# Transposing by VectorE blocks and GpSimd transfers in place of TensorE, halves-first FFN chunks, and keys and queries with the weights stationary, in a two-layer decoder trunk

## The reference

```
x = x + 0.5 * swiglu_ffn(rmsnorm(x, norm_ffn1[l]), ffn1_w_in[l], ffn1_w_out[l])      # 1024 -> 2 x 2816 -> 1024
z = rmsnorm(x, norm_mix[l]) @ mix_w_in[l]         # 2048 columns, split among four mixers A, B, C, D
x = x + concat(y_a, y_b, y_c, y_d) @ mix_w_out[l]
# cross attention, 4 heads of 256, 256 memory rows:
q = (rmsnorm(x, norm_xattn[l]) @ wq);  k, v = split(rmsnorm(mem, norm_mem[l]) @ wkv)
p = softmax(q k^T / sqrt(256));  x = x + (p v) @ wo
x = x + 0.5 * swiglu_ffn(rmsnorm(x, norm_ffn2[l]), ffn2_w_in[l], ffn2_w_out[l])
```

## Time and profile before

| | |
|---|---|
| median of 3 runs | 1118.09 us (1118.0 to 1118.31) |
| the profiled execution | 1116.31 us |
| its span | 1114.6 us |
| PE busy | 1101.6 us, 99% |
| DVE busy | 705.2 us, 63% |
| ACT busy | 541.7 us, 49% |
| POOL busy | 371.5 us, 33% |
| clock granted to TensorE | 1.0 but in the first and the last slice of 40 |

### The profile page before, as it was taken

One profiled execution on the slowest core, in us unless ns is written; L12 is line 12 of the kernel. 1 busy time (PEld: TensorE's weight loads), 2 busy tenths in 40 slices (PEclk: granted clock), 3 DMA queues, 4 the chain that ended last, 5 costly groups with the idle time before them and its releaser, 6 DMA issues.

```text
span 1114.6 us, 13351 instructions
## 1 busy us (share of the span) xinstructions
PE 1101.6 (99%) x4998; PEld 911.9 (82%) x4998; DVE 705.2 (63%) x811; ACT 541.7 (49%) x599; POOL 371.5 (33%) x727
## 2 busy tenths in 40 slices
PE   8999999999999999999999999999999999999996
PEld 7888888888888888888888888888888888888885
DVE  6666655799655655654565656468986557666552
ACT  6454534845554544443454535357464545444431
POOL 0686820000000056773017767000000002676610
PEclk9999999999999999999999999999999999999998
DMA  8977565644553477766567676556454436766561
GB/s 261 298 231 210 188 218 175 216 158 135 206 189 98 131 230 223 216 214 198 187 201 220 212 227 197 187 189 205 144 184 168 165 116 193 214 213 217 190 206 62
DMA packets 181792, 214.29 MB, mean 192 GB/s; under 512 B 18186, under 2 KB 137558, under 8 KB 181728
## 3 DMA queue, kind: packets, MB, share of 16 engines
q1 hardware_dynamic: 158112, 200.82, 55.8%
q0 software_dynamic: 22528, 11.58, 3.9%
q10 hardware_dynamic: 1088, 1.05, 0.3%
HBM read 200.79 MB, written 1.05 MB: 181 GB/s over the span
## 4 chain that ended last, share of the span: by engine, by line
PE 88%; issue 5%; ACT 2%; DVE 2%; DMA 1%; POOL 1%; DVEq 0%; SPq 0%; POOLq 0%; ACTq 0%
PE acc L1291 27%; PE acc L1293 27%; PE acc L1292 27%; PE turn L1189 3%; PE acc L1484 1%; PE acc L1459 1%; DMA w_raw<-in_ffn_w_in 1%; ACT w_hi L423 1%; DVE w_lo L751 1%; POOL kT L388 1%; DVE arena L955 1%; PE acc L1262 0%; PE acc L1386 0%; PE acc L1263 0%; PE acc L1273 0%
## 5 line engine op out<-in xcount | busy, mean ns | idle before, releaser
L751 DVE TENSOR_TENSOR w_lo<-w_raw,w_hi 128x2048 fp32r<-128x2048 f32 x191 | 428.0, 2246 | 231.4 <-ACT w_hi L423 231.2
L423 ACT CAST w_hi<-w_raw 128x2048 fp32r<-128x2048 f32 x191 | 357.2, 1871 | 128.7 <-PE acc L1293 114.8
L388 POOL DMA_DIRECT2D kT<-kT x704 | 344.2, 497 | 161.0 <-DVE kT L862 117.9
L1291 PE MATMUL acc<-w_hi,xT_hi 128*128 128x512 f32 x872 | 342.3, 393 | 0.0
L1293 PE MATMUL acc<-w_hi,xT_lo 128*128 128x512 f32 x872 | 339.7, 390 | 0.0
L1292 PE MATMUL acc<-w_lo,xT_hi 128*128 128x512 f32 x872 | 339.3, 389 | 0.0
L1291 PE MATMUL acc<-w_hi,hT_hi 128*128 128x512 f32 x608 | 240.7, 396 | 0.8 <-DVE hT_lo L940 0.8
L1293 PE MATMUL acc<-w_hi,hT_lo 128*128 128x512 f32 x608 | 237.1, 390 | 0.0
L1292 PE MATMUL acc<-w_lo,hT_hi 128*128 128x512 f32 x608 | 236.6, 389 | 0.0
L379 POOL TENSOR_TENSOR rstd<-var,mhalf 128x2 f32<-128x2 f32 x14 | 24.2, 1730 | 575.5 <-DVE var L788 428.1
L1293 PEld LDWEIGHTS acc<-w_hi,xT_lo 128*128 128x128 f32 x872 | 163.7, 188 | 34.6
(11 more groups left out here) (111 smaller groups left out, 500.8 us busy)
## 6 DMA issues: line engine op xcount, KB each, us to landing
w_raw<-in_ffn_w_in SPq DMA_DIRECT2D x174, 512.0 KB, 5.0
...
```

Of the source, the lines that this page charges most:

```text
L388: pool.dma_start(hfeat[B * q:B * q + B, g % 2, a * RUN:(a + 1) * RUN], hblk[B * a:B * a + B, g % 2, q * RUN:(q + 1) * RUN]).then_inc(hfeat ...
L423: act.copy(w_hi[:, u % SLOTS, 0:n], w_raw[:, u % SLOTS, 0:n]).then_inc(w_split_hi, 1)
L751: dve.tensor_tensor(w_lo[:, u % SLOTS, 0:n], w_raw[:, u % SLOTS, 0:n], w_hi[:, u % SLOTS, 0:n].bitcast(F32), ALU.subtract).then_inc(w_spli ...
L1291: pe.matmul(o, hi, wh, start=(first and j == 0), stop=False)
```

## The change

It has four parts.

1. **Twelve turns of the residual go** (`mi00`, `mi01`, `f2in10`, `f2in11` in both layers, `next00`, `next01`, and layer 1's `start10`, `start11`). In their place VectorE transposes `xs` in blocks (`x_blocks`), GpSimd issues 16 transfers of 32 rows of 1024 bytes (`x_shuffle`) for the half, and VectorE multiplies what landed by the gain (`gained_blocks`). `xblk` and `xfeat` are the memory that `hblk` and `hfeat` use, and waits keep them apart. The other boundary turns stay.
2. **Chunks 0 to 2 of an FFN go by halves**, but for the very first FFN: TensorE does half 0 of chunks 0, 1, 2 and then half 1 of each (`in_order`, `unit_of`; the loads follow). Each chunk's split of hidden features (`hidden_hi`, `hidden_lo`) comes one chunk later in the lists.
3. **Keys and queries are computed with the weights stationary** (`unit_t`): 48 matmuls of 256 columns instead of 24 of 512; the result has features on partitions, so the 16 turns of keys and queries and ScalarE's copies of them go. The second token tile of a half is needed with the first.
4. Since a row's scale can't be applied there any more, **the memory is scaled once at the start** (two VectorE operations in chunk 5 of the first FFN; the turns of `sgu_w` now stand ahead of the memory's), and the queries' scale goes into the softmax's scale (`qscale`) and its maximum.

```diff
+    def staged(l, f):
+        return (l, f) != (0, 0)
+
+    def unit_of(base, l, f, c, j):
+        if staged(l, f) and c < 3:
+            return base + 3 * j + c
+        return base + 2 * c + j
+
+    def in_order(l, f):
+        if staged(l, f):
+            return [(c, j) for j in range(2) for c in range(3)] + [(c, j) for c in range(3, FC) for j in range(2)]
+        return [(c, j) for c in range(FC) for j in range(2)]
...
     def layer_turns(l):
-        return ([f"start1{t}" for t in range(T)] + chunk_turns(l, 0) + [f"mi{n}{t}" for n, t in part]
-                + ["glu", "am", "b", "w", "u", "k00", "k01", "k10", "k11", "conv", "norm"]
-                + [f"q_in{n}{t}" for n, t in part] + ["q00", "q01", "q10", "q11"]
+        return (([] if l else [f"start1{t}" for t in range(T)]) + chunk_turns(l, 0) + [f"mi1{t}" for t in range(T)]
+                + ["glu", "am", "b", "w", "u", "conv", "norm"]
+                + [f"q_in{n}{t}" for n, t in part]
                 + ["p0", "p1", "p2", "p3"]
-                + [f"f2in{n}{t}" for n, t in part] + chunk_turns(l, 1)
-                + ([f"next0{t}" for t in range(T)] if l < L - 1 else []))
+                + [f"f2in0{t}" for t in range(T)] + chunk_turns(l, 1))
...
-        xT_hi = sb("xT_hi", [P, KT, S], F32R)
-        xT_lo = sb("xT_lo", [P, KT, S], F32R)
-        hT_hi = sb("hT_hi", [P, FT, S], F32R)
-        hT_lo = sb("hT_lo", [P, FT, S], F32R)
+        xT = sb("xT", [P, KT, 2, S], F32R)
+        hT = sb("hT", [P, FT, 2, S], F32R)
+        xT_hi, xT_lo = xT[:, :, 0, :], xT[:, :, 1, :]
+        hT_hi, hT_lo = hT[:, :, 0, :], hT[:, :, 1, :]
...
+        xblk, xfeat = kT[:, 0:4, :].rearrange("p k s -> p (k s)"), kT[:, 4:8, :].rearrange("p k s -> p (k s)")
...
+            def x_shuffle(h):
+
+                pool.wait_ge(xblk_ready, T * (h + 1))
+                pool.wait_ge(hT_ready, 1 + chunks_past(h))
+                if h:
+                    pool.wait_ge(xg_ready, xg_count(h - 1))
+                for a in range(NBLK):
+                    for q in range(NBLK):
+                        pool.dma_start(xfeat[B * q:B * q + B, a * XRUN:(a + 1) * XRUN],
+                                       xblk[B * a:B * a + B, q * XRUN:(q + 1) * XRUN]).then_inc(xfeat_landed, 16)
...
+                x_shuffle(x_half(l, 1, 0))
+                for k, i in enumerate((V_MIX, V_SGU, V_CLN, V_Q)):
                     inv_sqrt(at.at(6, 3 + k), i)
+                x_shuffle(x_half(l, 3, 1))
+                inv_sqrt(at.at(6, 7), V_F2)
                 for c in range(FC):
...
-                                       scale=rstd[:, V_MEM, t:t + 1]).then_inc(k_ready, 1)
-
-                def key_turn(n):
-                    for t in range(T):
-                        act.wait_ge(turned, turn_no(at.l, f"k{n}{t}"))
-                        act.copy(kT[:, 4 * n:4 * n + 4, t * P:(t + 1) * P],
-                                 tb[TB[f"k{n}{t}"]][:, :].rearrange("p (k s) -> p k s", k=4)).then_inc(kT_ready, 1)
+                    for c in range(2):
+                        evac(U_K + 2 * n + 1, c)
+                        act.copy(kT[:, 4 * n + 2 * c:4 * n + 2 * c + 2, :],
+                                 acc[KPAIR][c][:, :].rearrange("p (k s) -> p k s", k=2)).then_inc(kT_ready, 1)
...
-                    if (l, f) == (0, 0) and 3 <= c < 7:
+                    weights_to(base + (6 + c if staged(l, f) and c < 2 else 2 * c + 4), at)
...
+            def x_blocks(l, b, n, t):
+
+                h = x_half(l, b, n)
+                dve.wait_ge(x_updated, 16 * l + (T + 4 * (b - 1) + 2 * n + t + 1 if b else 2 * n + t + 1 - 2))
+                if h:
+                    dve.wait_ge(xfeat_landed, 16 * NBLK * NBLK * h)
+                for g in range(max(0, chunks_past(h) - 2), chunks_past(h)):
+                    dve.wait_ge(hfeat_landed[g % 2], hfeat_count(g))
+                dve.transpose(xblk.rearrange("p (q k t s) -> p t k q s", q=NBLK, k=4, t=T)[:, t, :, :, :],
+                              xs[:, t, n * GN:(n + 1) * GN].rearrange("p (k q s) -> p k q s", k=4, q=NBLK)).then_inc(xblk_ready, 1)
+
+            def gained_blocks(l, b, n, g):
+
+                h = x_half(l, b, n)
+                dve.wait_ge(xfeat_landed, 16 * NBLK * NBLK * (h + 1))
+                gain = par_all[:, l, g * KT + 4 * n:g * KT + 4 * n + 4].unsqueeze(2).unsqueeze(3).to_broadcast([P, 4, NBLK, B])
+                for t in range(T):
+                    dve.tensor_tensor(xg[:, t, :].rearrange("p (k a s) -> p k a s", k=4, a=NBLK),
+                                      xfeat.rearrange("p (a k t s) -> p t k a s", a=NBLK, k=4, t=T)[:, t, :, :, :],
+                                      gain, ALU.mult).then_inc(xg_ready, 1)

...
-                    split_lo(base + 2 * c + 5, at)
-                    if (l, f) == (0, 0) and c == 7:
+                    if c >= 2:
+                        hidden_lo(c - 2)
...
+                    if (l, f) == (0, 0) and c == 5:
+                        dve.wait_ge(rstd_ready, 2)
+                        for t in range(T):
+                            dve.tensor_scalar(mem_sb[:, t, :], mem_sb[:, t, :], rstd[:, V_MEM, t:t + 1], None, ALU.mult).then_inc(mem_scaled, 1)
...
+                    if b == 2:
+                        weights_to(u_end + 4, at)
+                        for t in range(T):
+                            update(b, 1, t, u_end + 2, pairs[1], factor, at)
+                            x_blocks(l, 3, 1, t)
+                        dve.wait_ge(x_squared, at.at(16, 8 + 4 * (b + 1)))
+                        variance(i_var, steps)
+                        weights_to(u_end + 6, at)
+                        gained_blocks(l, 3, 1, g)
+                        for t in range(T):
+                            xT_lo_part(b + 1, 1, t, at)
+                        return
...
-                    dve.tensor_scalar(nmax[:, h, :], smax[:, h, :], -SCALE, None, ALU.mult).then_inc(nmax_ready, 1)
+                    dve.scalar_tensor_tensor(out=nmax[:, h, :], in0=smax[:, h, :], scalar=-SCALE, in1=rstd[:, V_Q, :],
+                                             op0=ALU.mult, op1=ALU.mult).then_inc(nmax_ready, 1)
...
+            def unit_t(u, at, pair, s, k0, first, last, between=None):
+
+                pe.wait_ge(w_split, at.at(UNITS, SLOTS + u + 1))
+                slot = u % SLOTS
+                for c in range(GN // P):
+                    o = acc[pair][c // 2][:, (c % 2) * S:(c % 2 + 1) * S]
+                    for j in range(GK):
+                        cols = slice(j * GN + c * P, j * GN + (c + 1) * P)
+                        hi, lo = s[:, k0 + j, 0, :], s[:, k0 + j, 1, :]
+                        pe.matmul(o, w_hi[:, slot, cols], hi, start=(first and c % 2 == 0 and j == 0), stop=False, skip_group_check=True)
+                        pe.matmul(o, w_hi[:, slot, cols], lo, start=False, stop=False, skip_group_check=True)
+                        ins = pe.matmul(o, w_lo[:, slot, cols], hi, start=False, stop=(last and j == GK - 1), skip_group_check=True)
+                    if c % 2:
+                        ins.then_inc(unit_done, 1)
+                    if between and c == 1:
+                        between()
+
...
+            def staged_wait(b, c, j, at):
+
+                def acc_read(t):
+                    pe.wait_ge(x_updated, at.at(16, (T + 4 * (b - 1) if b else -T) + 2 + t + 1))
+
+                return xT_wait(b, j, at) if c == 0 else acc_read if (b, c, j) in ((0, 1, 0), (3, 2, 0)) else None
...
-                    unit(base + 1, at0, 0, xT_hi, xT_lo, GK, False, True, before=xT_wait(b, 1, at0))
-                for c in range(1, FC):
+                    for c, j in in_order(l, f)[:6]:
+                        unit(unit_of(base, l, f, c, j), at0, c, xT_hi, xT_lo, GK * j, j == 0, j == 1, before=staged_wait(b, c, j, at0))
+                for c in range(3 if staged(l, f) else 1, FC):
                     if (l, f, c) == (0, 0, 1):
...
-                        if n == 1 and j < 2 and (f == 0 or l < L - 1):
-                            x_turn(4 if f else 1, 0, j, f"next0{j}" if f else f"mi0{j}", at0)
...
-                mem_unit(U_K, KPAIR, 0, True)
+                unit_t(U_K, at, KPAIR, hT, MEM_KT, True, False)
                 pe.wait_ge(mT_ready, at.at(4, 4))
-                mem_unit(U_K + 1, KPAIR, GK, False)
+                unit_t(U_K + 1, at, KPAIR, hT, MEM_KT + GK, False, True)
...
-                def key_turns(n, free):
-                    for t in range(T):
-                        pe.wait_ge(k_ready, at.at(4, 2 * n + t + 1))
-                        free(t)
-                        turn(TB[f"k{n}{t}"], [(j * P, kbuf[:, t, j * P:(j + 1) * P]) for j in range(4)])
-
-                pe.wait_ge(k_ready, at.at(4, 2))
...
-                query_turn(0, 0)
-                query_turn(0, 1)
-                unit(U_Q + 3, at, QPAIR[1], xT_hi, xT_lo, GK, False, True)
+                pe.wait_ge(xT_ready, at.at(16, 4 * 2 + 2))
```

(12 more changed lines are left out.)

207 lines of the change are left out of this document (99 added, 108 removed).

## The result

The changed kernel takes 1126.97 us (median of 4 runs, 1126.54 to 1127.1) against 1118.05 (4 runs, 1116.24 to 1118.31): ratio 1.0086, 95% interval 1.0074 to 1.0097. It is slower by 0.86%; the forecast was 1115.3, faster. The profiled execution has a span of 1125.0 us where before had 1114.6.

A forecast was written before the change was run, and what follows sets the result against it. The prediction took the sum of TensorE's work to bound the kernel, with every wait counting in full. Its terms, 9.4 - 2.6 + 0.4 - 4.4 = 2.8 us less, took 1118.09 to 1115.3 us, range 1110 to 1127.

The forecast's parts named there:

- What bounds the kernel: Whole kernel: time is the sum of TensorE's work, any TensorE wait counts in full; VectorE also bounds one stage.
- Turns at 0.47 us: On TensorE: each turn taken away gains 0.47 us; twelve residual and eight query turns together 9.4 us.
- 256 columns at 0.120 us, 0.32 a unit: Keys' and queries' units: 48 matmuls at 0.120 us each cost 0.32 us more a unit, 2.6 us for eight units.
- Rival 1: Keys' and queries' matmuls: cost scales with columns, 0.113 down to 0.110 us each, giving 1112.7 to 1111.4 us; chance 0.18.
- rival 2: Keys' and queries' units: the weight load comes to bind; 1126.7 us at 0.136 us a matmul, about 1166 at 0.188; chance 0.12.
- Keys in VectorE's stage, 0.4 us let through: Mixers' stage: keys net 1.2 us gained, of which VectorE's cover of 0.22 us a layer lets 0.4 us through.
- q_in at 0: Queries' second unit needs both token tiles at its start: cost 0, with 0.3 us of cover.
- half 0 at 0: Half 0 of the mixers' and layer 1's way in: costs nothing, with 30 us of second output units over it.
- the memory's scale at 0: First FFN: scaling the memory takes VectorE 2.3 us but costs nothing; uncovered it would cost 2.3 us once.
- The new chain: Half 1 into FFN 2 (twice) and layer 1, by blocks and transfers: TensorE waits 1.3, 1.8 and 1.3 us, together 4.4.
- The sum: Whole kernel: 9.4 - 2.6 + 0.4 - 4.4 = 2.8 us less, a median of 1115.3 us.
- number 3: Half-1 exchanges: longer than their rows; 1139 us if 1024-byte rows double the issue, 1120 at a tenth; chance 0.08.

The follow-up runs named there:

- hold: The changed kernel, with SyncE loading the sixth unit of a halves-first FFN only after the half-1 exchange has landed: 1109.89 us, ratio 0.9935 to the kernel before.
- rows512: The changed kernel, with each of the 16 transfers of a half-1 exchange carrying only 512 bytes of each 1024-byte row: 1123.31 us, one run.

## Why the prediction was wrong, step by step

- **What bounds the kernel** (the sum of TensorE's work, every wait in full): right, and more than in full.
- **Turns at 0.47 us**: right. Twelve residual turns gave 5.8 us, 0.48 each.
- **256 columns at 0.120 us, 0.32 a unit**: right to the last digit. Queries: 1.25 us gained where 8 x 0.47 - 2.6 = 1.2 was said. Rival 1, the cost going with the columns, rival 2, the weight load binding, and the 262 cycles, 109 ns, of the Trainium skill are all out.
- **Keys in VectorE's stage, 0.4 us let through**: 0.6 came through; the wait at `y_lo` grew from 0.4 to 0.5, as said.
- **q_in at 0, half 0 at 0, the memory's scale at 0**: right; no wait shows at any of these places.
- **The new chain**: the frame was right. Updates and transposes took 2.75 us (2.6 said), GpSimd's delay 0.3 (0.3), issue 7.9 (7.8, by transfers and not bytes), gain to first matmul 2.2 (2.1). **The term that was mis-sized is the set of 16 transfers: 13.2 to 13.5 us where I took 11.4**, and that lay beyond my upper end of 13.0. Three times 1.8 to 2.1 us, and some 0.25 each from the small terms, are the 6.6 us between 4.4 and 11.0. The error was in how the row was picked: I took the middle one of 44 sets, while they scatter between 8.9 and 13.0, and I did not ask what makes them scatter. I should have asked what SyncE loads behind this set: two `w_lo` in a row, at 385.01 and on, free two slots, and 2 MB of weights go out just as the last transfers do. hold shows the same set at 9.06 us. The trace of before could have told it. In the records of its DMA packets, six of the 44 sets have less than 10 GB/s of loads behind their last issue, and their last packet lands 0.8 us behind it; the other 38, with 32 to 313 GB/s, take 1.4 to 4.2 us. Below are windows of before from the last issue to the last packet, for the sets that took 8.9, 13.0 and 11.9 us (in the first, the 40 GB/s are the set's own):

```profile
597.52:598.35 0.83, 0.83 (x6) 0.67 (x5) 0.83 (x3) 0.07 (x1) 0.00 (x0) 1.00 0.17 40
105.36:109.27 3.91, 3.91 (x19) 3.25 (x18) 3.27 (x3) 0.00 (x0) 0.35 (x1) 1.00 0.74 217
405.26:408.20 2.94, 2.94 (x14) 2.44 (x13) 2.71 (x2) 0.00 (x0) 0.01 (x1) 1.00 0.58 188
```

- **The step that was not there at all** is the clock behind a wait. I priced each wait by its length. The three cost 11.0 and then 5.7 more, half as much again. Behind its start TensorE never waits longer than 0.4 us in before, so no row had it at such a place; but the timeline of before has the lower level too: the first unit's matmuls start 0.43 us apart until 12.4 us, behind a start with little to do, and 0.23 from 12.7. The Trainium skill has it ("TensorE: Matmul & The Clock Gate", section HAM oscillation — how this bites in real kernels): waits for a DMA between stretches of matmuls bring the clock down, and the next stretch begins slow. The trace of after agrees at its three waits: 0.43 us a matmul behind them, 0.23 elsewhere. It did not happen behind every such wait in the experiments (below).
- **The sum**: -5.8 - 1.25 - 0.6 = -7.6 us for the work, where -7.2 was said. With waits of 11.0 and the clock's 5.7 it is +9.1, and the medians moved by 8.9. The start's 1.2 us are not in this sum. That 1126.97 lies within the range given, 1110 to 1127, is luck: the upper end was rival 2's price for weight loads, and the starts of 0.120 us rule that rival out.
- **The rivals**: number 3 was the one, "the exchange longer than its rows", at 0.08. It had bigger rows for its cause, which rows512 rules out, and no clock, and its prices, 1139 and 1120, are not what came. A row that scatters by half of its value, on a chain that releases the engine that bounds the kernel, deserved more than that.
